# A fused transformer step on one core: coefficients of the expert rows computed on one engine instead of two

## The chip, the core and the metric

The kernel runs on one core of one Trainium2 chip, in fp32 throughout. A core has five engines that run side by side and meet only through semaphores: TensorE (PE in the profile) multiplies matrices, VectorE (DVE) and ScalarE (ACT) do elementwise work, GpSimd (POOL) here only issues gathers, and SyncE (SP) issues the other transfers. 16 DMA engines carry all transfers. The metric is the device time of one execution in microseconds (us), median of three runs.

## The reference, cut to what matters

One layer of a decoder trunk for 512 prompt tokens and 8 sample tokens: projections, retention and block-sparse attention, cross-attention over 256 memory tokens, and then the part that fills two thirds of the time, the retrieval of single-neuron experts. Each token has 8 heads, each head picks 16 of 16384 experts, and each expert is one row of `u` and one of `v`, 1024 numbers each:

```python
top, sel = lax.top_k(cand, PEER_TOPK)
expert = jnp.take_along_axis(cidx, sel, axis=-1)
g = jax.nn.softmax(top, axis=-1)
act = jax.nn.gelu(jnp.einsum('cd,chkd->chk', xc, u[expert]).astype(jnp.float32))
return jnp.einsum('chk,chkd->cd', (g * act).astype(v.dtype), v[expert])
```

So for each token and each picked expert there is a dot product `s` with the `u` row, a coefficient g·gelu(s), and the `v` row is added with that coefficient. gelu is the tanh form: 0.5·s·(1 + tanh(0.79788·(s + 0.044715·s³))).

## The kernel before, in words

Tokens lie on the 128 partitions, in four prompt tiles and one sample tile of 8. `u` and `v` are stored side by side, so one indirect DMA (line 759) brings, for one slot (head and rank) and all 128 tokens of a tile, the `u` and the `v` row of each token's expert: 128 rows of 8 KB, 1 MB in all. There are 4·128 such gathers for the prompt and 8 for the sample tile, 520 in all. They land in a ring of 7 buffers, `ring[k]`. GpSimd issues them strictly in order, and a gather waits until the previous user of its buffer has raised `row_free[k]`.

The program is written as a loop over 260 pairs of gathers, `PAIRS`, in the same order on every engine. x counts the 8 pairs of a head from 0 to 7. For pair p, before the change:

- VectorE takes the two dot products of pair p (`dot`, line 2266; each is one instruction over 128x1024 and a short one that reads the sum out), and raises `dots_done` after the second.
- ScalarE squares the two sums (`pair_gelu`, line 1550), VectorE forms s·(1 + 0.044715·s²) and s times half the gate (`pair_argument`, lines 2272 and 2275), ScalarE takes the tanh (line 1553), and VectorE forms the coefficients (`pair_coefs`, line 2282). That last step stands behind the first dot product of pair p+1 in VectorE's program.
- The `v` rows are added on two engines. Of the 8 ranks in each half head, slots 0, 2, 4, 5 and 7 (`PE_ROWS`) go to TensorE, the others to VectorE. For TensorE, ScalarE scales an identity matrix by the coefficients (`value_weights`, line 1565) into one of 6 buffers, and TensorE multiplies it with the row in four matmul instructions (line 1338: two halves of 512 columns, and an fp32 matmul is two instructions), summing in PSUM. For VectorE it is one instruction over 128x1024 (`value_rows`, line 2300) that adds into `h`. Pairs x = 2 and x = 6 of a head have two TensorE rows, the others one of each kind.
- After 64 pairs a tile is complete, and `add_sum` (line 2312) adds the PSUM sum to `h`. TensorE's first row of the next tile waits for that.

Around the pairs each engine has two other streams. Between the dot products VectorE takes pieces of the routing of later heads (`take`), that is the top-16 searches. And behind every odd pair, each engine takes the next piece of a background program (`advance(steps, progress(p // 2))`): the rest of the attention for the sample tokens and for the last prompt tile. On these pieces ScalarE mostly copies what TensorE has put in PSUM, and TensorE waits for the copy, so the two work in step there. The background ends about two thirds of the way through the pairs. In the program of TensorE, pair p-1's rows and then the background piece stand in iteration p; in that of ScalarE, it is the scaled identities of pair p-1, then square and tanh of pair p, and then the background piece.

## Time and profile before

| what | us |
|---|---|
| median of three runs | 2437.39 (2437.17 to 2438.58) |
| the profiled execution, its own time | 2440.81 |
| its span, first to last instruction | 2439.0 |
| first expert gather issued at | 748.80 |
| DVE busy / PE busy / POOL busy / ACT busy | 1460.5 / 1732.5 / 720.9 / 517.3 |

The profiled execution is 1.8 us longer than its span and 3.4 us above the median of the runs. The page's slices show three regions: the projections and the prompt's attention up to about 740 us, the pairs with background work up to about 1850 us, and the pairs with little beside them but routing up to the end. Busy time is the time in which an engine has an instruction in work; waiting for a semaphore is not counted.

### The profile page before, as it was taken

Reading aid. Unit: us, or ns where it says so; the run is one execution under the profiler, and the core shown is the slowest. Engines: PE = TensorE matmul, PEld = TensorE weight load, DVE = VectorE, ACT = ScalarE, POOL = GpSimd, SP = SyncE. Lnnn points to the kernel's source line nnn. Section 1 sums busy time; section 2 is a strip of 40 time slices with the busy share of each in tenths; the row PEclk is TensorE's granted clock in tenths of the full one; section 3 lists DMA queues with packets and bytes.
Section 4 is the critical chain, followed back from the end, with each engine's and each line's share of the span. In section 5 each row is a group of like instructions: output and inputs, shape, how many; then the busy total and the mean of one; then the engine's idle time right before and its main releaser. Section 6 shows DMA issues by size and latency. Waiting matters only on the chain.

```text
span 2439.0 us, 19114 instructions
## 1 busy us (share of the span) xinstructions
PE 1732.5 (71%) x5401; PEld 815.7 (33%) x5401; DVE 1460.5 (60%) x4222; ACT 517.3 (21%) x1533; POOL 720.9 (30%) x560
## 2 busy tenths in 40 slices
PE   5999998789783795796466666775765655566565
PEld 2333775435451231443122322441431222122221
DVE  2200037611215767547956785766877899999876
ACT  2000234512320231121112122111121211111212
POOL 0000000000005335423422343333433455554542
PEclk9999968989795898677778888777886667777778
DMA  6110600053018879968896997988999998999997
GB/s 211 69 69 35 205 6 1 20 179 141 1 67 312 306 297 390 374 255 293 308 384 278 388 374 297 364 349 335 385 374 403 375 366 348 358 368 381 374 401 294
DMA packets 124976, 654.41 MB, mean 268 GB/s; under 512 B 22960, under 2 KB 34256, under 8 KB 56928
## 3 DMA queue, kind: packets, MB, share of 16 engines
q0 software_dynamic: 78016, 562.07, 59.0%
q1 hardware_dynamic: 41816, 82.86, 9.9%
q10 hardware_dynamic: 5040, 8.26, 1.0%
q8 instruction: 44, 0.72, 0.1%
q14 instruction: 60, 0.49, 0.1%
HBM read 642.78 MB, written 14.55 MB: 270 GB/s over the span
## 4 chain that ended last, share of the span: by engine, by line
PE 41%; DMA 19%; issue 16%; DVE 13%; POOL 7%; ACT 4%; SPq 1%; ACTq 0%; POOLq 0%; DVEq 0%
DMA arena<-in_peer_uv,expert 17%; PE bank L1338 12%; PE bank L804 9%; POOL arena L759 6%; DVE arena L2266 3%; PE bank L1004 3%; DVE arena L2300 2%; PE bank L1089 2%; PE bank L1194 2%; PE bank L1228 2%; PE bank L1070 1%; PE bank L1121 1%; POOL arena L735 1%; PE bank L1205 1%; PE bank L826 1%
## 5 line engine op out<-in xcount | busy, mean ns | idle before, releaser
L1338 PE MATMUL bank<-arena 128*128 128x512 f32 (+1 forms) x1312 | 849.8, 797 | 579.9 <-ACT arena L1565 536.0
L759 POOL DMA_INDIRECT arena<-in_peer_uv,expert x512 | 671.4, 1311 | 946.9 <-PE bank L1338 785.9
L2266 DVE CUSTOM_DVE_ANT_0 arena<-arena 128x1024 f32<-128x1024 f32 x520 | 635.1, 1221 | 272.6 <-DMA arena<-in_peer_uv,expert 263.0
L1338 PEld LDWEIGHTS bank<-arena 128*128 128x128 f32 (+1 forms) x1312 | 300.1, 246 | 1104.8 <-issue 1104.3
L2300 DVE SCALAR_TENSOR_TENSOR arena<-arena 128x1024 f32<-128x1024 f32 x192 | 244.2, 1272 | 0.5
L804 PE MATMUL bank<-arena 128*128 128x512 f32 (+3 forms) x560 | 227.5, 565 | 0.0
L1565 ACT ACTIVATE arena<-arena 128x128 f32<-128x128 f32 x320 | 121.5, 399 | 407.1 <-DVE arena L2282 405.3
L1550 ACT ACTIVATE arena<-arena 128x2 f32<-128x2 f32 x260 | 53.1, 204 | 638.8 <-DVE arena L2266 638.8
L735 POOL DMA_INDIRECT arena<-in_cache_slc_k,row_idx x16 | 15.1, 946 | 444.0 <-DMA sc_scores<-arena 439.4
L804 PEld LDWEIGHTS bank<-arena 128*128 128x128 f32 (+1 forms) x560 | 93.6, 169 | 133.4 <-issue 128.3
L1763 DVE TENSOR_TENSOR arena<-arena 128x256 f32<-128x256 f32 (+5 forms) x20 | 6.4, 320 | 197.2 <-ACT arena L1411 197.2
L2272 DVE SCALAR_TENSOR_TENSOR arena<-arena 128x2 f32<-128x2 f32 x260 | 39.9, 153 | 79.4 <-ACT arena L1550 77.6
L1004 PE MATMUL bank<-arena 128*128 128x512 f32 (+1 forms) x160 | 72.3, 611 | 14.7 <-DMA arena<-in_w_out 12.0
L1553 ACT ACTIVATE arena<-arena 128x2 f32<-128x2 f32 x260 | 53.3, 205 | 123.9 <-DVE arena L2272 123.8
L728 POOL DMA_INDIRECT arena<-in_cache_cmp_k,blk_idx x2 | 2.0, 1023 | 243.0 <-PE bank L804 243.0
L2137 DVE MAX8 arena<-arena 128x8 f32<-128x128 f32 (+3 forms) x120 | 35.9, 326 | 48.8 <-ACT arena L1533 48.2
L1411 ACT ACTIVATE arena<-bank 128x512 f32<-128x512 f32 (+3 forms) x35 | 20.0, 570 | 207.6 <-PE bank L804 207.6
L1089 PE MATMUL bank<-arena 128*128 128x384 f32 (+1 forms) x256 | 58.2, 383 | 1.2 <-ACT arena L1391 1.2
L1968 DVE TENSOR_REDUCE arena<-bank 128x1 f32<-128x256 f32 (+1 forms) x17 | 7.2, 423 | 86.2 <-PE bank L1031 81.0
L1194 PE MATMUL bank<-arena 64*64 64x512 f32 x96 | 50.9, 614 | 0.5 <-ACT arena L1641 0.5
L1089 PEld LDWEIGHTS bank<-arena 128*128 128x128 f32 x256 | 40.6, 191 | 22.6 <-issue 5.7
L785 PE MATMUL bank<-arena 128*128 128x128 f32 (+1 forms) x136 | 23.6, 325 | 32.6 <-DVE arena L1746 27.8
(283 smaller groups left out, 1938.7 us busy)
## 6 DMA issues: line engine op xcount, KB each, us to landing
arena<-in_w_in SPq DMA_DIRECT2D x6, 2048.0 KB, 7.7
arena<-in_w_out SPq DMA_DIRECT2D x2, 4096.0 KB, 23.6
arena<-in_peer_uv,expert POOLq DMA_INDIRECT x512, 8.9
arena<-in_w_mq SPq DMA_DIRECT2D x2, 2048.0 KB, 10.7
arena<-in_peer_wq SPq DMA_DIRECT2D x2, 2048.0 KB, 10.7
arena<-in_w_mo SPq DMA_DIRECT2D x2, 2048.0 KB, 17.5
sc_scores<-arena ACTq DMA_DIRECT2D x4, 1024.0 KB
arena<-in_cache_mem_k SPq DMA_DIRECT2D x2, 2048.0 KB, 11.0
```

The lines of the kernel that those rows point to most:

```text
L759: pool.indirect_dma_start(out=ring[k], out_offset=None, in_=a["peer_uv"], in_offset=bass.IndirectOffsetOnAxis(ap=idx, axis=0)).then_inc(ro ...
L804: ins = pe.matmul(bank[0:R, 0:w], hnT[:, k, t * P:t * P + R], w_last[:, k, :] if last else w_buf[:, i % 2, k, 0:w], start=(k == 0), stop=( ...
L1004: ins = pe.matmul(bank[0:R, :], grp.catT[t][:, k, 0:R], grp.w_out[:, k, half * 512:(half + 1) * 512], start=(k == 0), stop=(k == KC - 1))
L1089: ins = pe.matmul(bank[:, 0:grp.width], grp.wq[:, k, hh * P:(hh + 1) * P], grp.hnT[:, k, :], start=(k == 0), stop=(k == KC - 1))
L1194: ins = pe.matmul(banks[4 + cc][0:64, :], q_mask[0:HD, bg, :], keyT[0:HD, gi % 2, :], start=(bg == 0), stop=(bg == BG - 1))
L1228: ins = pe.matmul(bank[0:HD, bg * R4:(bg + 1) * R4], vals[:, bg, j * HD:(j + 1) * HD], s_probsT[:, j, bg * R4:(bg + 1) * R4], start=(j == ...
L1338: ins = pe.matmul(banks[b + half][0:R, :], weights, ring[k][:, D + half * 512:D + (half + 1) * 512], start=first, stop=last)
L1550: act.activation(gelu_w[:, c0:c0 + 2], act_p[:, c0:c0 + 2], ACT.Square, scale=GELU_A ** 0.5).then_inc(act_squared, 1)
L1553: act.activation(gelu_w[:, c0:c0 + 2], gelu_w[:, c0:c0 + 2], ACT.Tanh, scale=GELU_B).then_inc(gelu_tanh, 1)
L1565: act.activation(diag[:, d % DIAGS, :], ident, ACT.Copy, scale=coef[:, slot:slot + 1]).then_inc(diag_ready, 1)
L2266: return dve.tensor_tensor_reduce(out=ring[k][:, 0:D], in0=ring[k][:, 0:D], in1=other, scale=1.0, scalar=0.0, op0=ALU.mult, op1=ALU.add, a ...
L2300: stt(out=h[:, n // H, :], in0=ring[k][:, D:2 * D], scalar=coef[:, c:c + 1], in1=h[:, n // H, :], op0=ALU.mult, op1=ALU.add).then_inc(row_ ...
```

## The change

The whole chain from dot products to coefficients moves to ScalarE. Square and tanh stay as instructions over two columns. The products with per-token factors become activations over one column each, with a column of SBUF as scale, and where something is added, as bias: the product s·half_gate is Copy with scale half_gate; s·(1 + 0.044715·s²) is Identity of the square with scale s and bias s; the coefficient is Identity of the tanh with scale and bias s·half_gate. That is 8 ScalarE instructions for a pair in place of 2, with four waits of ScalarE for its own results (`coef_step`, `coef_ready`), and none on VectorE in place of 3.

ScalarE then makes the scaled identities of the same pair at once, and TensorE's rows of pair p stand in iteration p and no longer in p+1. VectorE's rows stand where they did, behind the first dot product of the next pair. For the sample pairs the masked weights `coef_m` are made on ScalarE too. `add_sum` comes after pair x = 0 of the next tile and no longer after x = 1. `gates_made` tells ScalarE that the gates of a head are there.

```diff
@@ TensorE
-                    pe.wait_ge(diag_ready, diags[0])
+                weighted[0] += 1
+                pe.wait_ge(diag_ready, weighted[0])
...
-                if p:
-                    pair_values(p - 1, *PAIRS[p - 1])
+                pair_values(p, n, x)
                 if p % 2:
                     advance(steps, progress(p // 2))
-            pair_values(p, n, x)
@@ ScalarE
-            def pair_gelu(p, n, x):
+            def pair_coefs(p, n, x):
                 c0 = n % H * TOPK + 2 * x if n < HEADS else SLOTS + 2 * x
+                each = [slice(c, c + 1) for c in (c0, c0 + 1)]
+                if x == 0:
+                    act.wait_ge(gates_made, n + 1)
                 act.wait_ge(dots_done, p + 1)
-                act.activation(gelu_w[:, c0:c0 + 2], act_p[:, c0:c0 + 2], ACT.Square, scale=GELU_A ** 0.5
-                               ).then_inc(act_squared, 1)
-                act.wait_ge(gelu_in, p + 1)
-                act.activation(gelu_w[:, c0:c0 + 2], gelu_w[:, c0:c0 + 2], ACT.Tanh, scale=GELU_B
-                               ).then_inc(gelu_tanh, 1)
+                mark(act.activation(gelu_w[:, c0:c0 + 2], act_p[:, c0:c0 + 2], ACT.Square, scale=GELU_A ** 0.5))
+                for c in each:
+                    ins = act.activation(gated_x[:, c], act_p[:, c], ACT.Copy, scale=half_gate[:, c])
+                mark(ins)
+                act.wait_ge(coef_step, marks[0] - 1)
+                for c in each:
+                    ins = act.activation(gelu_w[:, c], gelu_w[:, c], ACT.Identity, scale=act_p[:, c], bias=act_p[:, c])
+                mark(ins)
+                act.wait_ge(coef_step, marks[0])
+                mark(act.activation(gelu_w[:, c0:c0 + 2], gelu_w[:, c0:c0 + 2], ACT.Tanh, scale=GELU_B))
+                act.wait_ge(coef_step, marks[0])
+                for c in each:
+                    ins = act.activation(coef[:, c], gelu_w[:, c], ACT.Identity, scale=gated_x[:, c], bias=gated_x[:, c])
+                ins.then_inc(coef_ready, 1)
...
-                if p:
-                    value_weights(p - 1, *PAIRS[p - 1])
-                pair_gelu(p, n, x)
+                pair_coefs(p, n, x)
+                value_weights(p, n, x)
@@ VectorE (pair_argument and pair_coefs are removed)
                 if x == 0 and n % H == 0 and 0 < n < HEADS:
                     t = n // H
+                    dve.wait_ge(dots_done, p)
...
-                if p:
-                    pair_coefs(p - 1, *previous)
                 take(before + (x + 0.5) * share)
                 if p:
                     value_rows(p - 1, *previous)
...
-                pair_argument(p, n, x)
                 previous = (n, x)
-                if n % H == 0 and 0 < n < HEADS and x == 1:
+                if n % H == 0 and 0 < n < HEADS and x == 0:
                     add_sum(n // H - 1)
```

ScalarE's program at a piece of background work in which it copies four banks of transposed keys for TensorE (line 1641 before, 1660 after; one row of x8 is two such pieces), before the change. L1550 is the square, L1553 the tanh, L1565 a scaled identity:

```order
L1550 ACTIVATE arena<-arena 128x2 [waits dots_done]
L1553 ACTIVATE arena<-arena 128x2 [waits gelu_in]
L1641 ACTIVATE arena<-bank 64x512 [waits s_keyT_done] x8
L1565 ACTIVATE arena<-arena 128x128 [waits row_free6,coef_ready]
L1550 ACTIVATE arena<-arena 128x2 [waits dots_done]
L1553 ACTIVATE arena<-arena 128x2 [waits gelu_in]
```

The same place after it. L1556 is the square, L1558 the product with the gate, L1562 the argument, L1565 the tanh, L1568 the coefficient, L1584 the scaled identity:

```order
L1556 ACTIVATE arena<-arena 128x2 [waits dots_done]
L1558 ACTIVATE arena<-arena 128x1 x2
L1562 ACTIVATE arena<-arena 128x1 [waits coef_step]
L1562 ACTIVATE arena<-arena 128x1
L1565 ACTIVATE arena<-arena 128x2 [waits coef_step]
L1568 ACTIVATE arena<-arena 128x1 [waits coef_step]
L1568 ACTIVATE arena<-arena 128x1
L1584 ACTIVATE arena<-arena 128x128 [waits row_free6,coef_ready]
L1660 ACTIVATE arena<-bank 64x512 [waits s_keyT_done] x8
```

The scaled identity of the odd pair stood behind the background copies and now stands ahead of them; the next pair's whole chain now stands behind them.

VectorE's program at the start of the third prompt tile, before the change. L2266 is a dot product, L2272, L2275 and L2282 are the small steps, L2300 is a row of VectorE, L2312 is `add_sum`:

```order
L2272 SCALAR_TENSOR_TENSOR arena<-arena 128x2 [waits act_squared]
L2275 TENSOR_TENSOR arena<-arena 128x2 [waits gate_step]
L2266 ISA arena<-arena 128x1024 [waits row_in6]
L2266 ISA arena 128x1
L2282 SCALAR_TENSOR_TENSOR arena<-arena 128x2 [waits gate_step,gelu_tanh]
L2148 MAX arena<-arena 128x8 [waits route_step]
L2148 MAX arena<-arena 128x8
L2300 SCALAR_TENSOR_TENSOR arena<-arena 128x1024 [waits row_free2,coef_ready]
...
L2312 TENSOR_TENSOR arena<-arena,bank 128x512 [waits row_free3,row_free2]
```

The same place after it, where L2283 is the dot product, L2297 VectorE's row and L2309 `add_sum`:

```order
L2309 TENSOR_TENSOR arena<-arena,bank 128x512 [waits row_free3,row_free2]
L2309 TENSOR_TENSOR arena<-arena,bank 128x512
L2283 ISA arena<-arena 128x1024 [waits row_in6]
L2283 ISA arena 128x1
L2165 MAX arena<-arena 128x8 [waits route_step]
L2165 MAX arena<-arena 128x8
L2297 SCALAR_TENSOR_TENSOR arena<-arena 128x1024 [waits row_free2,coef_ready]
```

The three small steps are gone, and `add_sum` stands ahead of the dot product into buffer 6 and no longer behind that of buffer 0.

## Rows read from the trace of the kernel before

**Rows 1.** Windows view; busy us per engine, clock, DMA share, GB/s of two stretches.

```profile
740.00:1850.00 1110.00, 744.58 (x2171) 335.41 (x2171) 765.56 (x2148) 216.10 (x706) 417.63 (x343) 0.78 0.87 339
1850.00:2345.00 495.00, 298.50 (x438) 106.20 (x438) 450.93 (x1393) 87.11 (x316) 260.46 (x174) 0.73 0.97 372
```

**Rows 2.** Waits, 740 to 1850: engine, line, awaited; us in total, times, longest.

```profile
POOL arena L759 <- PE bank L1338: 575.6, 140, 32.2
ACT arena L1565 <- DVE arena L2282: 262.5, 127, 17.4
DVE arena L2266 <- DMA arena<-in_peer_uv,expert: 213.5, 131, 30.1
DVE arena L2272 <- ACT arena L1550: 72.6, 15, 15.6
ACT arena L1553 <- DVE arena L2272: 63.8, 154, 1.4
```

**Rows 3.** Waits, 1850 to 2345.

```profile
POOL arena L759 <- PE bank L1338: 201.0, 78, 13.5
ACT arena L1565 <- DVE arena L2282: 123.8, 85, 3.4
ACT arena L1553 <- DVE arena L2272: 56.8, 85, 1.2
DVE arena L2266 <- DMA arena<-in_peer_uv,expert: 37.3, 48, 2.3
```

**Rows 4.** Timeline, one pair late on: start us, us, engine, instruction.

```profile
2224.74 0.20 ACT L1550 ACTIVATE arena<-arena 128x2 f32<-128x2 f32 x1 [2.60 <-DVE arena L2266]
...
2225.64 0.14 DVE L2275 TENSOR_TENSOR arena<-arena 128x2 f32<-128x2 f32 x1
2225.71 1.21 DVE L2266 CUSTOM_DVE_ANT_0 arena<-arena 128x1024 f32<-128x1024 f32 x1
...
2226.86 0.14 DVE L2282 SCALAR_TENSOR_TENSOR arena<-arena 128x2 f32<-128x2 f32 x1
2226.93 0.74 DVE L2188 TENSOR_TENSOR arena<-arena 8x256 f32<-8x256 f32 x2
2227.04 0.69 ACT L1565 ACTIVATE arena<-arena 128x128 f32<-128x128 f32 x2 [1.09 <-DVE arena L2282]
```

**Rows 5.** ScalarE: line 1380, an activation over one column, min/median/max ns.

```profile
L1380 ACT ACTIVATE arena<-arena x22: 293/294/296, 23.5 to 2434.0; 128x1 f32<-128x1 f32 x18, 8x1 f32<-8x1 f32 x4
```

**Rows 6.** Timeline, two turns with background work between TensorE and ScalarE.

```profile
881.32 5.68 PE L1338 MATMUL bank<-arena 128*128 128x512 f32 x12
...
886.84 0.60 PE L1205 MATMUL bank<-arena 128*64 128x128 f32 x4
...
892.15 0.59 ACT L1641 ACTIVATE arena<-bank 64x512 f32<-64x512 f32 x1 [0.96 <-PE bank L1205]
892.64 0.39 ACT L1565 ACTIVATE arena<-arena 128x128 f32<-128x128 f32 x1
892.93 0.19 ACT L1550 ACTIVATE arena<-arena 128x2 f32<-128x2 f32 x1
893.18 3.97 PE L1338 MATMUL bank<-arena 128*128 128x512 f32 x8
893.35 0.20 ACT L1553 ACTIVATE arena<-arena 128x2 f32<-128x2 f32 x1 [0.23 <-DVE arena L2272]
893.46 0.20 ACT L1540 ACTIVATE arena<-arena 128x16 f32<-128x16 f32 x1
```

**Rows 7.** Timeline, the start of the second tile.

```profile
1215.81 0.15 DVE L2272 SCALAR_TENSOR_TENSOR arena<-arena 128x2 f32<-128x2 f32 x1
...
1225.83 5.08 PE L1338 MATMUL bank<-arena 128*128 128x512 f32 x8 [10.43 <-DVE arena L2312]
```

**Rows 8.** Chain that ended last: start us, us, what; the two longest background pieces shown.

```profile
1021.96 27.41 PE bank L1228 x256
...
1639.40 15.03 PE bank L1070 x32
```

More of the change, by code:

```diff
@@ L498, in trunk_kernel @@
         route_step = sem("route_step")
-        act_squared = sem("act_squared")
+        coef_step = sem("coef_step")
+        gates_made = sem("gates_made")
         gate_step = sem("gate_step")
-        gelu_in = sem("gelu_in")
-        gelu_tanh = sem("gelu_tanh")
         x_done = sem("x_done")
@@ L1316, in background @@
                 yield STEPS_DONE
-            diags = [0]
+            diags, weighted = [0], [0]
             def value_row(p, n, x, y):
@@ L1327, in value_row @@
                     weights, first, last = coef_m[:, j, :], j == 0, j == DB - 1
-                    pe.wait_ge(coef_ready, p + 1)
                 else:
@@ L1545, in sample_exp, with mark @@
                 act.activation(best_v[0:DB, :], best_v[0:DB, :], ACT.Exp).then_inc(sample_gate, 1)
-            def pair_gelu(p, n, x):
+            marks = [0]
+            def mark(ins):
+                ins.then_inc(coef_step, 1)
+                marks[0] += 1
+            def pair_coefs(p, n, x):
                 c0 = n % H * TOPK + 2 * x if n < HEADS else SLOTS + 2 * x
+                each = [slice(c, c + 1) for c in (c0, c0 + 1)]
+                if x == 0:
+                    act.wait_ge(gates_made, n + 1)
@@ L1556, in _ @@
+                act.wait_ge(coef_step, marks[0])
+                for c in each:
+                    ins = act.activation(coef[:, c], gelu_w[:, c], ACT.Identity, scale=gated_x[:, c], bias=gated_x[:, c])
+                ins.then_inc(coef_ready, 1)
             diags, diag_user = [0], []
             def value_weights(p, n, x):
+                act.wait_ge(coef_ready, p + 1)
                 for y in range(2):
-                    if n < HEADS and PE_PART[n, x, y]:
+                    if n == HEADS:
+                        j = 2 * x + y
+                        act.activation(coef_m[:, j, :], eye8[:, j, :], ACT.Copy, scale=coef[:, SLOTS + j:SLOTS + j + 1]
+                                       ).then_inc(diag_ready, 1)
+                    elif PE_PART[n, x, y]:
@@ L1561, in value_weights @@
                         d, slot = diags[0], n % H * TOPK + 2 * x + y
-                        act.wait_ge(coef_ready, p + 1)
                         if d >= DIAGS:
@@ L1724, in _ @@
                     mean_square(h[0:DB, SAMPLE, :], hn3[:, SAMPLE, :], x_done, 1)
-            value_weights(p, n, x)
             mean_square(h[:, PT - 1, :], hn3[:, 3, :], sum_added, 2 * PT)
@@ L2226, in sample_columns @@
                 dve.wait_ge(rt_done, 1)
-                order(dve.tensor_copy(half_gate[:, SLOTS:SLOTS + DB], banks[0][:, DB:2 * DB]))
+                dve.tensor_copy(half_gate[:, SLOTS:SLOTS + DB], banks[0][:, DB:2 * DB]).then_inc(gates_made, 1)
                 dve.tensor_copy(expert_s[:, :], banks[0][:, 0:DB]).then_inc(idx_ready, 1)
@@ L2232, in final_norm @@
                 normed(h[:, t, :], h[0:R, t, :], gain[:, 0, :]).then_inc(y_ready, 1)
-            gates, x_marked = [0], {}
+            gates = [0]
             def gate_mark(ins):
@@ L2252, in head_gates @@
                 dve.wait_ge(gate_step, gates[0])
-                gate_mark(ts(half_gate[:, cols], best_e[:, cols], scale, None, ALU.mult))
+                ts(half_gate[:, cols], best_e[:, cols], scale, None, ALU.mult).then_inc(gates_made, 1)
                 yield
@@ L2267, in dot @@
                                                 scalar=0.0, op0=ALU.mult, op1=ALU.add, accum_out=act_p[:, c:c + 1])
-            def pair_argument(p, n, x):
-                cols = pair_cols(n, x)
-                dve.wait_ge(act_squared, p + 1)
-                stt(out=gelu_w[:, cols], in0=gelu_w[:, cols], scalar=1.0, in1=act_p[:, cols], op0=ALU.add, op1=ALU.mult
-                    ).then_inc(gelu_in, 1)
-                dve.wait_ge(gate_step, gates[0])
-                gate_mark(tt(gated_x[:, cols], act_p[:, cols], half_gate[:, cols], ALU.mult))
-                x_marked[p] = gates[0]
-            def pair_coefs(p, n, x):
-                cols = pair_cols(n, x)
-                dve.wait_ge(gelu_tanh, p + 1)
-                dve.wait_ge(gate_step, x_marked[p])
-                ins = stt(out=coef[:, cols], in0=gelu_w[:, cols], scalar=1.0, in1=gated_x[:, cols], op0=ALU.add, op1=ALU.mult)
-                if n == HEADS:
-                    order(ins)
-                    ins = tt(coef_m[:, 2 * x:2 * x + 2, :], eye8[:, 2 * x:2 * x + 2, :],
-                             coef[:, cols].unsqueeze(2).broadcast_to((P, 2, DB)), ALU.mult)
-                ins.then_inc(coef_ready, 1)
             last_row = []
@@ L2380, in _ @@
                     final_norm(SAMPLE)
-            pair_coefs(p, *previous)
             value_rows(p, *previous)
```

## The prediction, made before the changed kernel ran

> **What bounds the kernel now.** I read the page first: the projections and the prompt's attention, up to 740 us, are untouched, so I cut the rest into stretches with the windows view [rows 1]. The first stretch, 740 to 1850, holds some 158 pairs (316 of the 343 GpSimd instructions, the others being page gathers of the attention), 7.0 us each; no engine is full (DVE 69%, PE 67%) and the DMA engines moved 339 GB/s. The second, 1850 to 2345, holds 87 pairs (174 gathers), 5.7 us each, with VectorE busy 451 of 495 us and the DMA engines at 0.97 and 372 GB/s. Then the waits. In the first stretch GpSimd waited 576 us for TensorE to free a ring buffer, and VectorE 214 us for gathers to land [rows 2]: the ring is the bound, a circle of gather, dot products, coefficients, TensorE's row, next gather. Seven buffers at 3.5 us a row make a circle of 24.6 us. In the second stretch VectorE lost only 37 us to gathers [rows 3]: there it is the bound itself, with a nearly full DMA right behind it.
>
> In that circle the part that the change touches is the time from square to scaled identity. From the waits: 0.20 (square) + wait of the tanh for VectorE + 0.20 (tanh) + wait of the identity for VectorE. Second stretch: 0.20 + 56.8/85 + 0.20 + 123.8/85 = 2.5 us [rows 3]; the pair shown has 2.30, of which 1.2 us is the first dot product of the next pair, standing ahead of the coefficients [rows 4]. First stretch: 0.20 + 63.8/154 + 0.20 + 262.5/127 = 2.9 us [rows 2], and more for an odd pair, whose identity stands behind a background piece as well.
>
> **The new chain, step by step.** Neither an activation over one column with two column operands nor ScalarE waiting for itself stands in the trace. Line 1380 takes one column operand over one column: 294 ns [rows 5]. An activation over two columns without one takes 200 [rows 4], so a column operand adds some 90, and I take 385 for two. Independent activations start about 0.1 us before the one ahead ends (893.35 + 0.20 against 893.46 [rows 6]). A dependent one I start 0.05 after the end. Then: square to 0.20; two Copies started at 0.11 and 0.30, to 0.59; two Identities at 0.49 and 0.77, to 1.15; tanh 1.20 to 1.40; two Identities at 1.45 and 1.73, to 2.11; identity matrix at 2.15. Bounds: if column operands cost nothing it is about 1.25; with no overlap anywhere, 0.2 + 0.59 + 0.77 + 0.2 + 0.77 + 0.2 of handing over = 2.75. I take 2.15.
>
> The Trainium skill says the same of the operands (ScalarE: Activation LUTs, What ACT_TABLE_LOAD costs): an activation with immediate scale and bias takes 186 ns and each pointer operand adds about 93. By that page the two-operand form would take an estimated 373 ns and the chain about 2.1 us. It speaks against the change: the chain is longer in instruction time than the old one, and only its place is better.
>
> So the chain is about 0.4 us shorter than the average old one in the second stretch, and at most level with the shortest old ones.
>
> **What it is worth, place by place.**
>
> *VectorE's three small steps.* They start 0.07 us apart and the next instruction 0.07 behind [rows 4], so each takes 0.07 from the engine and not its 0.15: 0.21 us a pair. In the second stretch, where VectorE is the bound, 87 x 0.21 = 18 us. VectorE's row needs the coefficients 2.11 after the square; it reaches that place after the next first dot, which in the pair shown ended 2.2 after it, and a routing piece of up to 0.75 more [rows 4]. So there is no new stall on average, but only 0.1 to 0.8 of margin. Gathers then have to run at 372 x 5.7/5.5 = 386 GB/s. I take 18, and bound it by 0 (DMA full already) and 18 + 37 (landing waits gone as well). Of those 37 us, an earlier release by 0.4 in a circle of 20 us gives back some 5. Second stretch: -23.
>
> *Tile starts, three.* TensorE's first row waited for `add_sum`, which stood behind the second pair: idle 10.4 us at 1225.8 [rows 7]. The first pair's argument was formed at 1215.8; now its coefficients are there at about 1217, and `add_sum` (two instructions of 0.7 us) runs at 1215.8 to 1217.1. So the row starts some 8 us sooner. The ring covers part of that; I take 5 us each, -15 in all, between 0 and 3 x 8.
>
> *First stretch, release of odd pairs.* The odd pair's rows now come ahead of the background piece on both engines. For an identity that waited behind it the gain is 2 us or more; averaged with the even pairs, which gain little, 1.1 us in a circle of 24.6 us, 4.5%. Over some 800 us of the stretch, 1110 less 12 turns of 12 us [rows 6] and seven of about 24, this is -36 us, bounded by 0 and, if every wait of VectorE for a gather went, by 214.
>
> *First stretch, turns in which TensorE and ScalarE work in step.* Here the change costs. In the turn shown the rows of three slots take 5.7 us, the background piece 6.3, and TensorE is never idle: its next row starts 0.5 us after ScalarE's last copy, since the odd pair's coefficients were made by VectorE meanwhile [rows 6]. Now the pair behind the piece is an even one whose whole chain stands behind ScalarE's copies: TensorE idles 2.15 us more. There are 12 such pieces of key copies (16·8/4 + 16·4/4 = 48 copies of line 1641, in fours): +26. Behind the long pieces, of which I count seven in the code's steps (the two shown took 27 and 15 us on TensorE [rows 8]), the same chain is exposed: +15. Also, each piece now starts on TensorE later against the dot products (behind pair p's rows instead of pair p-1's), so ScalarE is held longer. VectorE no longer stops at the next square for that (72.6 us in 15 waits [rows 2]) but at the next row, some 3 us further on; I set the one against the other, at 0.
>
> *VectorE's small steps in the first stretch* lie beside its waits for gathers: 0, at best 158 x 0.21 = 33.
>
> *The end.* Behind the last dot products nothing hid the old chain, 0.2 + 0.15 + 0.2 + 0.15 and four hand-overs, 0.9 us; now 2.15: +1.
>
> Sum: -23 - 15 - 36 + 26 + 15 + 1 = -32. The profiled span of 2439.0 would become 2407, its execution 2409, and the median, 3.4 us lower than that execution, **2405**.
>
> **Rivals.**
>
> *A larger gain.* The ring is the bound of the first stretch and everything on it counts in full: the exposed chains are covered by the extra pair in flight, the small steps give 33 there, and the landing waits shrink. -23 - 24 - 36 - 33 + 1 = -115 at the most; half way from my sum, **2365**. For it speak the 576 us that GpSimd waited for TensorE [rows 2]. Against it speak the DMA engines at 0.87 already.
>
> *No change.* In the second stretch the DMA engines are full at 0.97 [rows 1], so VectorE's gain becomes landing wait, and the first stretch's gains and costs meet at zero: within 5 us of **2437**. Against it speaks that no stretch has shown a sharp limit at 372 GB/s.
>
> *Slower.* One mechanism: ScalarE is held in a background piece until TensorE has done pair p's rows and the piece, and the next pair's coefficients begin only then. Before, the piece could start while pair p's dot products were still running. It starts now 2.65 us (chain and identity) and a row of 1.9 us or more behind them, some 4 us later. The pair period is 7 us; once a piece takes more than about 2.5 us, the next square is late and TensorE idles for the chain in every such turn. If it decides in 40 of the 79 turns and not in 12, it costs 40 x 2.15 = 86 in place of 26, and the odd pairs' gain is used up too (the even pair is late by as much): -23 - 15 + 86 + 15 + 1 = +64, less what the ring absorbs, about half: **2469**. It would decide from about 25 turns on. The even distribution of small pieces speaks for it, against it that the ring holds three and a half pairs.
>
> That the change does not do what it says is little likely: the order on each engine shows the chain and the moved rows. Identity is not among the functions that the kernel used; the number of table loads in the order is unchanged.
>
> **How the numbers follow.** The forecast has 0.46, the larger gain 0.20, no change 0.11, slower 0.23. The forecast's own range is 2385 to 2428. The range of 2368 to 2462 leaves out the outer half of the larger gain and a part of the slower case. A difference under 0.2% (5 us) is about what a measurement of this kernel can't tell from none. Faster: 0.46 x 0.98 + 0.20 = 0.65. Within: 0.12. Slower: 0.23.
>
> **What would show it.** In the profile after: square to scaled identity 2.1 to 2.2 us in all but background turns, with the two-operand activations near 385 ns; VectorE's 3 x 260 small instructions gone; its period in the second stretch 5.4 to 5.5 us a pair, at 380 GB/s or more; a new wait of line 2297 for ScalarE, under 10 us in the second stretch; TensorE's wait for `add_sum` at the tile starts nearly gone; in the background turns TensorE idle some 2.7 us behind the last copy. The forecast is wrong if the first stretch is more than 10 us longer than before, if the new wait of VectorE for coefficients passes 40 us in all, or if the second stretch keeps its 5.7 us a pair.

## The result and the profile after

| | before | changed |
|---|---|---|
| median, us | 2437.96 (2437.17 to 2438.58, 4 runs) | 2509.1 (2499.19 to 2521.07, 4 runs) |
| ratio | | 1.0309, 95% interval 1.0268 to 1.0351 |
| span of the profiled execution | 2439.0 | 2511.2 |

The change makes the kernel 3.1% slower, where 1.3% faster was forecast; the time also lies outside the range. All ratios here and below compare executions in the chip's usual state; one of the kernel before, in the second set of experiments, took 3176 us at a lower granted clock and is left out.

The first look is at where the 72 us of the span arose. I take the end of the second dot product of each pair as a clock: pair 0 ends at 759.4 us before and 752.8 after, pair 160 at 1863.5 and 1947.1, pair 240 at 2323.1 and 2394.1, pair 256 at 2407.7 and 2480.2. So 90 us were lost over the 160 pairs with background work, and 12.5 us were won over the 80 pairs behind them. Pair 0 is 6.6 us sooner, which says nothing of the change: over all runs of this document it ends between 752.6 and 765.0.

The same stretches in the windows view of the changed kernel (columns as in [rows 1]):

```profile
740.00:1850.00 1110.00, 720.25 (x1984) 321.07 (x1985) 680.22 (x1566) 433.71 (x1528) 383.13 (x314) 0.75 0.81 311
1850.00:2345.00 495.00, 293.10 (x554) 112.96 (x553) 425.45 (x1124) 221.50 (x826) 247.38 (x171) 0.78 0.97 376
```

ScalarE has over twice the work. TensorE, VectorE, GpSimd and the DMA engines (311 GB/s in place of 339) are all less busy in the first stretch than before: nobody there is fuller but ScalarE, at 39%, and everyone waits more. The stretch also holds fewer pairs than before. Over the same pairs, 0 to 160, the first number behind the comma is TensorE's busy time; first before, then the changed kernel:

```profile
759.40:1863.50 1104.10, 753.53 (x2187) 338.87 (x2187) 773.43 (x2166) 218.42 (x714) 410.26 (x334) 0.79 0.87 341
```

```profile
752.80:1947.10 1194.30, 778.33 (x2187) 350.76 (x2187) 735.97 (x1687) 473.66 (x1674) 409.45 (x335) 0.76 0.82 316
```

The same 2187 TensorE instructions take 25 us more, at a granted clock of 0.76 in place of 0.79, and TensorE is idle for 416 us in place of 351. Those 25 and 65 us are the 90. The waits of the changed kernel, 740 to 1850 us, against [rows 2]:

```profile
POOL arena L758 <- PE bank L1337: 529.4, 131, 29.1
PE bank L1337 <- ACT arena L1584: 382.9, 105, 40.6
DVE arena L2283 <- DMA arena<-in_peer_uv,expert: 183.5, 106, 29.2
POOL arena L758 <- DVE arena L2297: 142.1, 22, 28.6
DVE arena L2297 <- ACT arena L1568: 130.6, 25, 18.1
```

Two rows of the kernel before that belong beside them, from the same view:

```profile
PE bank L1338 <- ACT arena L1565: 325.9, 105, 41.7
POOL arena L759 <- DVE arena L2300: 42.0, 15, 9.3
```

And 1850 to 2345 us, against [rows 3]:

```profile
POOL arena L758 <- PE bank L1337: 189.8, 77, 8.7
DVE arena L2283 <- DMA arena<-in_peer_uv,expert: 55.3, 55, 11.8
DVE arena L2297 <- ACT arena L1568: 9.7, 4, 5.2
```

The new wait is that of VectorE's row (line 2297) for coefficients that ScalarE had not made: 131 us in 25 waits in the first stretch, where VectorE used to lose 73 us in 15 waits at the square [rows 2], and 10 us in the second. GpSimd waits for VectorE's rows 142 us, before 42. TensorE's wait for scaled identities, the largest that it has, grew from 326 to 383 us.

The new chain itself came out as worked out. One pair in the stretch without background, to be read against [rows 4]; L1556 is the square, L1558 two products, L1562 two arguments, L1565 the tanh, L1568 two coefficients, L1584 the scaled identity:

```profile
2135.15 0.21 ACT L1556 ACTIVATE arena<-arena 128x2 f32<-128x2 f32 x1 [4.04 <-DVE arena L2283]
2135.26 0.46 ACT L1558 ACTIVATE arena<-arena 128x1 f32<-128x1 f32 x2
2135.63 0.65 ACT L1562 ACTIVATE arena<-arena 128x1 f32<-128x1 f32 x2
2136.31 0.21 ACT L1565 ACTIVATE arena<-arena 128x2 f32<-128x2 f32 x1
2136.55 0.66 ACT L1568 ACTIVATE arena<-arena 128x1 f32<-128x1 f32 x2
2137.24 0.40 ACT L1584 ACTIVATE arena<-arena 128x128 f32<-128x128 f32 x1
```

2.09 us from square to identity, 2.15 predicted; the median over pairs 158 to 244 is 2.10. The two forms with two column operands (min/median/max ns), against [rows 5]:

```profile
L1562 ACT ACTIVATE arena<-arena x520: 370/372/380, 753.8 to 2496.8; 128x1 f32<-128x1 f32 x174
L1568 ACT ACTIVATE arena<-arena x520: 370/380/389, 754.8 to 2497.7; 128x1 f32<-128x1 f32 x174
```

What went wrong is in a turn with background work. The timeline of the changed kernel, to be read against [rows 6]; L1204 is the start of TensorE's piece of key transposes, L1660 ScalarE's copies, the last of a piece shown:

```profile
896.65 0.59 ACT L1660 ACTIVATE arena<-bank 64x512 f32<-64x512 f32 x1 [0.97 <-PE bank L1204]
897.15 0.19 ACT L1556 ACTIVATE arena<-arena 128x2 f32<-128x2 f32 x1
...
899.78 8.33 PE L1337 MATMUL bank<-arena 128*128 128x512 f32 x12 [2.16 <-ACT arena L1584]
...
907.95 0.60 PE L1204 MATMUL bank<-arena 128*64 128x128 f32 x4
...
913.26 0.59 ACT L1660 ACTIVATE arena<-bank 64x512 f32<-64x512 f32 x1 [0.97 <-PE bank L1204]
913.75 0.19 ACT L1556 ACTIVATE arena<-arena 128x2 f32<-128x2 f32 x1
915.83 0.40 ACT L1584 ACTIVATE arena<-arena 128x128 f32<-128x128 f32 x1
915.83 1.28 DVE L2297 SCALAR_TENSOR_TENSOR arena<-arena 128x1024 f32<-128x1024 f32 x1 [10.10 <-ACT arena L1568]
916.38 3.43 PE L1337 MATMUL bank<-arena 128*128 128x512 f32 x4 [2.16 <-ACT arena L1584]
```

From first row to first row the turn takes 16.6 us; before it took 11.9 (881.32 to 893.18, [rows 6]). TensorE idles 2.16 us for a whole chain behind the piece, as the prediction priced it, but the three rows also take 8.3 us in place of 5.7. The windows view of the two turns (PEclk is the third number from the end) says more; first before, then the changed kernel:

```profile
881.30:893.20 11.90, 11.76 (x37) 4.42 (x37) 8.22 (x25) 4.07 (x11) 7.18 (x5) 1.00 0.84 310
```

```profile
899.70:916.40 16.70, 14.46 (x37) 5.61 (x37) 4.43 (x10) 7.34 (x25) 4.15 (x4) 0.81 0.77 291
```

Before, TensorE worked through the turn and had the full clock, 1.00; now it stands idle once and does part of the turn at the lower of its two levels. The first 3.2 us behind the idle time, in which it is busy throughout:

```profile
899.80:903.00 3.20, 3.20 (x4) 1.47 (x5) 1.08 (x1) 2.42 (x10) 0.00 (x0) 0.50 0.64 269
```

2.2 us of idle time and 2.6 us of slower rows make the 4.7 us of this turn. In the same turn VectorE stood for 10.1 us at its row, with the next dot products behind it.

Over all pairs up to 155, a square starts more than 0.3 us after its dot products 16 times before and 39 times in the changed kernel, and these delays add up to 78 and 231 us. Before, TensorE never stood idle for more than 0.1 us ahead of the first row of such a late pair. In the changed kernel it does so 24 times, for 1.7 to 6.1 us and 64 us in all: these are nearly the whole of the 65 us of added idle time.

### The profile page after: what moved, and what is told of

The parts are those of the page before. It is cut to its first block, busy times and chain, and to the rows that moved or that the text cites. A ratio compares the mean times of both kernels' runs of the same rounds, so it can differ in the third digit from the quotient of the medians.

```text
span 2511.2 us, 19608 instructions
## 1 busy us (share of the span) xinstructions
PE 1740.5 (69%) x5401; PEld 819.3 (33%) x5401; DVE 1399.0 (56%) x3438; ACT 933.5 (37%) x3101; POOL 710.7 (28%) x560
## 4 chain that ended last, share of the span: by engine, by line
PE 44%; DMA 16%; DVE 14%; ACT 10%; issue 10%; POOL 5%; SPq 1%; ACTq 0%; POOLq 0%; DVEq 0%
PE bank L1337 14%; DMA arena<-in_peer_uv,expert 13%; PE bank L803 9%; DVE arena L2283 5%; POOL arena L758 4%; DVE arena L2297 3%; PE bank L1003 3%; PE bank L1088 2%; ACT arena L1562 2%; PE bank L1193 2%; PE bank L1069 1%; PE bank L1227 1%; ACT arena L1568 1%; ACT arena L1558 1%; PE bank L1020 1%
## 5 line engine op out<-in xcount | busy, mean ns | idle before, releaser
L1337 PE MATMUL bank<-arena 128*128 128x512 f32 (+1 forms) x1312 | 864.4, 812 | 645.1 <-ACT arena L1584 636.6
L2283 DVE CUSTOM_DVE_ANT_0 arena<-arena 128x1024 f32<-128x1024 f32 x520 | 634.5, 1220 | 284.8 <-DMA arena<-in_peer_uv,expert 273.6
L1337 PEld LDWEIGHTS bank<-arena 128*128 128x128 f32 (+1 forms) x1312 | 307.7, 250 | 1177.5 <-issue 1177.1
L2297 DVE SCALAR_TENSOR_TENSOR arena<-arena 128x1024 f32<-128x1024 f32 x192 | 244.6, 1274 | 143.3 <-ACT arena L1568 143.0
L1556 ACT ACTIVATE arena<-arena 128x2 f32<-128x2 f32 x260 | 52.8, 203 | 721.6 <-DVE arena L2283 691.0
L1568 ACT ACTIVATE arena<-arena 128x1 f32<-128x1 f32 x520 | 172.8, 379 | 8.7
L1562 ACT ACTIVATE arena<-arena 128x1 f32<-128x1 f32 x520 | 169.0, 372 | 0.0
L734 POOL DMA_INDIRECT arena<-in_cache_slc_k,row_idx x16 | 15.1, 946 | 437.2 <-DMA sc_scores<-arena 432.6
L803 PEld LDWEIGHTS bank<-arena 128*128 128x128 f32 (+1 forms) x560 | 93.6, 169 | 133.4 <-issue 128.3
L1584 ACT ACTIVATE arena<-arena 128x128 f32<-128x128 f32 x320 | 121.9, 400 | 8.3
L1558 ACT ACTIVATE arena<-arena 128x1 f32<-128x1 f32 x520 | 120.8, 279 | 0.0
L1003 PE MATMUL bank<-arena 128*128 128x512 f32 (+1 forms) x160 | 71.5, 605 | 14.6 <-DMA arena<-in_w_out 11.9
L1565 ACT ACTIVATE arena<-arena 128x2 f32<-128x2 f32 x260 | 53.3, 205 | 8.0
L1660 ACT ACTIVATE arena<-bank 64x512 f32<-64x512 f32 x48 | 28.2, 592 | 75.1 <-PE bank L1204 75.1
```

Source lines behind the costliest of these rows:

```text
L803: ins = pe.matmul(bank[0:R, 0:w], hnT[:, k, t * P:t * P + R], w_last[:, k, :] if last else w_buf[:, i % 2, k, 0:w], start=(k == 0), stop=( ...
L1003: ins = pe.matmul(bank[0:R, :], grp.catT[t][:, k, 0:R], grp.w_out[:, k, half * 512:(half + 1) * 512], start=(k == 0), stop=(k == KC - 1))
L1337: ins = pe.matmul(banks[b + half][0:R, :], weights, ring[k][:, D + half * 512:D + (half + 1) * 512], start=first, stop=last)
L1558: ins = act.activation(gated_x[:, c], act_p[:, c], ACT.Copy, scale=half_gate[:, c])
L1562: ins = act.activation(gelu_w[:, c], gelu_w[:, c], ACT.Identity, scale=act_p[:, c], bias=act_p[:, c])
L1565: mark(act.activation(gelu_w[:, c0:c0 + 2], gelu_w[:, c0:c0 + 2], ACT.Tanh, scale=GELU_B))
```

## The experiments

Theory A: what costs is the order against the background, a chain exposed behind each piece. Theory B: the ScalarE chain costs wherever it stands. The kernel before ran beside each set below on that set's chip: medians of 2432.4, 2431.1 and 2434.7 us for the three sets, with single runs spread wider (2416 to 2449) than in the result above. So kernels of different sets are compared by their ratios. Where a text counts time from pair to pair, it is that of one profiled execution of each kernel.

**Only TensorE's piece moved back.** In the changed kernel:

```diff
@@ TensorE
+                if p % 2:
+                    advance(steps, progress(p // 2))
                 pair_values(p, n, x)
-                if p % 2:
-                    advance(steps, progress(p // 2))
```

> The changed kernel, with TensorE's background piece of an odd pair ahead of that pair's rows again (ScalarE unchanged: chain and scaled identities, then its piece). Theory A (order): the loss of the changed kernel sits where TensorE's piece, behind pair p's rows, starts only after pair p's dot products and chain, so that ScalarE is held and the next pair's whole chain is exposed behind the piece. Then this kernel gives the 90 us of the background stretch back and keeps the 13 us won in the stretch without background: 2410 to 2430 us, late squares back from 39 to about 16. Theory B (load and length): the 2.1 us chain of 8 ScalarE instructions itself costs, wherever TensorE's pieces stand: 2480 us or more.

Measured: 2442.6 us, ratio 1.0032 (1.0000 to 1.0064). That is 13 us above the range that I expected, but nearly the whole loss is gone by moving one engine's piece back ahead of the rows. Squares that start over 0.3 us after their dot products, 16 before and 39 in the changed kernel, are 22, and TensorE stands idle behind them 5 times in place of 24.

**The ScalarE chain with identities and TensorE's rows in the old place.**

```diff
@@ TensorE
+                if p:
+                    pair_values(p - 1, *PAIRS[p - 1])
-                pair_values(p, n, x)
@@ ScalarE
+                if p:
+                    value_weights(p - 1, *PAIRS[p - 1])
                 pair_coefs(p, n, x)
-                value_weights(p, n, x)
```

> The chain is on ScalarE, but scaled identities and TensorE's rows of pair p stand in iteration p+1, so behind the background piece of an odd pair on both engines, as before the change. Theory A: 2415 to 2435 us, a little slower than the kernel with only TensorE's piece moved, since the identity of an odd pair is late by the piece. Theory B: 2480 us or more.

Measured: 2434.7 us, ratio 1.0003 (0.9975 to 1.0031). Two turns of TensorE in its trace, the counterpart of the two above:

```profile
885.41 1.96 PE L1337 MATMUL bank<-arena 128*128 128x512 f32 x4
887.80 3.67 PE L1337 MATMUL bank<-arena 128*128 128x512 f32 x8 [0.43 <-ACT arena L1586]
891.31 0.60 PE L1204 MATMUL bank<-arena 128*64 128x128 f32 x4
...
897.64 1.96 PE L1337 MATMUL bank<-arena 128*128 128x512 f32 x4
```

The row behind the piece is that of the odd pair, whose coefficients were made ahead of the piece. The turn takes 12.2 us and the clock stays up, at 1.00: three rows in 5.6 us. ScalarE does all the work here that it does in the changed kernel, so Theory B is out. Against the kernel before, this one is 16 us late by pair 96 and makes it up again: from pair 160 to 240 it takes 444.9 us, before 459.6, changed kernel 447.1. But the run above, whose chain is the same too, takes 454.0, and the one with only the earlier sum, below, takes 453.2 with the old chain. So what the new chain wins in the late stretch is not told well by single executions: 6 to 15 us against before, and nothing clear against the run with the earlier sum.

**The piece ahead of the pair on both engines.** ScalarE's `advance` also moves ahead of `pair_coefs(p, n, x)`.

> The changed kernel, with the background piece ahead of the pair on both TensorE and ScalarE, so that the chain of the odd pair stands behind the piece instead of that of the even pair. Theory A in its narrow form (what costs is a whole chain behind a piece, with TensorE idle for it once in every background turn): little better than the changed kernel, 2450 to 2490 us, and clearly slower than the kernel with only TensorE's piece moved. If only the late start of the piece on TensorE costs, 2410 to 2430 us as there. Theory B: 2480 us or more.

Measured: 2527.1 us, ratio 1.0384 (1.0339 to 1.0428), slower than I expected of it and no better than the changed kernel. Here TensorE's piece starts as early as before the change, and only the chain stands behind it (now that of the odd pair; 42 late squares). So the late start of the piece is not the cause by itself: what counts is that no pair's coefficients are ready when the piece ends. TensorE stands idle behind such a late pair 39 times, for 125 us in all, against 24 times and 64 us in the changed kernel.

**Only the earlier tile sum**, in the kernel before: `x == 1` becomes `x == 0` at `add_sum`.

> The kernel before, with the one edit that the tile sums are added after pair x = 0 instead of x = 1. The prediction's step: 5 us at each of three tile starts, 2420 to 2430 us. Rival: TensorE's rows and the gathers behind them are covered by the ring, or wait for the coefficients as before, since these still stand behind the next pair's first dot product: 2435 to 2440 us.

Measured: 2430.3 us, ratio 0.9979 (0.9952 to 1.0006). Not told apart from no change; the 15 us (0.994) of the prediction are outside the interval. TensorE's idle time ahead of the first rows of the three tiles shrank from 10.4, 15.1 and 9.1 us to 4.4, 9.8 and 5.5 here, 15 us in all, and the time by some 5 at the median. In the changed kernel the idle time at the second tile's start did shrink, from 10.43 us [rows 7] to 2.13:

```profile
1258.03 1.27 DVE L2309 TENSOR_TENSOR arena<-arena,bank 128x512 f32<-128x512 f32 x2
1259.25 0.40 ACT L1584 ACTIVATE arena<-arena 128x128 f32<-128x128 f32 x1
1259.80 2.88 PE L1337 MATMUL bank<-arena 128*128 128x512 f32 x4 [2.13 <-ACT arena L1584]
```

With theory A shown in the main, the question was why the new chain wins so little elsewhere, and what its length is worth.

**A short chain in the changed kernel.** The coefficients are not the reference's here:

```diff
-                for c in each:
-                    ins = act.activation(gated_x[:, c], act_p[:, c], ACT.Copy, scale=half_gate[:, c])
+                ins = act.activation(gated_x[:, c0:c0 + 2], act_p[:, c0:c0 + 2], ACT.Copy)
...
-                for c in each:
-                    ins = act.activation(gelu_w[:, c], gelu_w[:, c], ACT.Identity, scale=act_p[:, c], bias=act_p[:, c])
+                ins = act.activation(gelu_w[:, c0:c0 + 2], gelu_w[:, c0:c0 + 2], ACT.Copy, scale=0.5)
...
-                for c in each:
-                    ins = act.activation(coef[:, c], gelu_w[:, c], ACT.Identity, scale=gated_x[:, c], bias=gated_x[:, c])
+                ins = act.activation(coef[:, c0:c0 + 2], gelu_w[:, c0:c0 + 2], ACT.Copy, scale=0.001)
```

> The changed kernel with its chain cut short: the six activations over one column with column operands become three over two columns with none (Copy in place of the product with the gate, of the argument and of the coefficient), so the coefficients are not the reference's; order, waits and everything else stay. The chain falls from 2.1 to about 1.0 us. Theory A (a whole chain stands behind each background piece): 39 late turns by 1.1 us give back about 43 us of the 84 lost in the background stretch, 2455 to 2475 us; what stays is the late start of TensorE's piece. If the length hardly counts: 2495 us or more. If it is all: 2430 us or less.

Measured: 2407.1 us, ratio 0.9893 (0.9860 to 0.9926): 4.2% off the changed kernel's ratio, 101 us, over twice what I expected, and more than all of the loss. The chain is 0.94 us, for instance:

```profile
2136.91 0.20 ACT L1556 ACTIVATE arena<-arena 128x2 f32<-128x2 f32 x1 [4.39 <-DVE arena L2280]
...
2137.85 0.40 ACT L1581 ACTIVATE arena<-arena 128x128 f32<-128x128 f32 x1
```

**The same short chain in the old place.**

> The same short chain (wrong coefficients again) in the kernel that has its scaled identities and TensorE's rows in the old place. With the full chain that kernel was level with before: about 16 us lost over the heavy background turns and 15 won in the stretch without background. If the loss there is the chain's length on ScalarE, the short chain gives it back: 2405 to 2420 us. If the stretch without background is bound by the ring, its period falls below the 5.56 us a pair of the full chain, to about 5.4; if by the DMA engines, it stays within 0.05 of it.

Measured: 2369.9 us, ratio 0.9757 (0.9715 to 0.9799). 1.15 us less of chain saves 2.5%, 60 us, where no piece stands between: not only the 16 us of the background turns that I expected, but something in every pair. From pair 160 to 240 it takes 431.0 us, 5.39 a pair against 5.56, and VectorE has the same work in both. In the changed kernel's order the short chain wins as much there, 434.2 against 447.1. So VectorE alone did not set the period.

**The old chain while there is background, the changed one behind it** (pairs 0 to 155 and 156 to 259; with the earlier tile sum).

> The old two-engine chain in its old place for pairs 0 to 155, as long as there is background work, and the changed chain, in its new place, for pairs 156 to 259; tile sums a pair sooner throughout. Theory A: no loss in the background stretch, the 13 us of the stretch without background and some 3 of the earlier sum: 0.992 to 0.996 of the kernel before, about 2415 to 2422 us where that has 2432. If the gain of the late stretch in the changed kernel was only that of a kernel that had fallen behind (other transfers out of the way): 0.999 to 1.002.

Measured: 2423.1 us, ratio 0.9958 (0.9934 to 0.9982). The changed chain where no background is behind it, with the earlier tile sum, makes the kernel 0.4% faster, about 10 us, as expected. In its profiled execution 7.1 us of it came between pairs 160 and 240, but the kernel with only the earlier sum is 6.4 us ahead of before in the same pairs. What the chain won there, and what the earlier sum, is not shown.

**Six ring buffers in place of seven**, in the kernel before (`RING = 6`). Theory C, which the expectations name from here on: the ring's circle of gather, dot products, coefficients and row sets the period in the late stretch too.

> The kernel before with 6 ring buffers in place of 7. Theory C: the circle of gather, dots, coefficients, row is of fixed length, so the period grows by up to 7/6: from 5.7 to 6.3 to 6.6 us a pair in the stretch without background, and the whole by 120 us or more. My prediction's reading, that VectorE is the bound there: the period stays within 5.9 us, and the whole grows by under 60 us, from the first stretch.

Measured: 2639.1 us, ratio 1.0838 (1.0784 to 1.0891). From pair 160 to 240 it takes 525.2 us, 6.57 a pair against 5.75: times 1.143, where 7/6 would be 1.167. In the windows view its stretch 1850 to 2345 has VectorE at 379 us and 326 GB/s; below it, for comparison, the short chain in the old place:

```profile
1850.00:2345.00 495.00, 273.70 (x528) 108.01 (x526) 379.01 (x1162) 75.80 (x276) 184.59 (x147) 0.75 0.88 326
```

```profile
1850.00:2345.00 495.00, 303.62 (x475) 105.61 (x474) 441.50 (x1122) 133.93 (x617) 266.73 (x184) 0.78 0.99 396
```

Three and a half pairs of 5.75 make a circle of 20.1 us, three of 6.57 make 19.7. So the circle sets the period with six buffers, and with seven it is as long as the period too. That it is then the only bound does not follow. The circle is not of fixed length either: the time from square to identity grew from 2.6 to 3.35 us late on, since the coefficients stand behind the next pair's first dot product, and VectorE's dot products waited 111 us for gathers in this stretch, before 37 [rows 3]. And 1.15 us less of chain would by the ring alone give 1.15/3.5 = 0.33 us a pair; 0.17 came late on, and 0.23 over all 260 pairs. VectorE's work, the gathers and the ring are close to balance there. Nor was 0.97 a full DMA: 396 GB/s are to be had.

**A chain shared by what is short where.** Square on ScalarE and argument and gate product on VectorE, as before the change; then tanh and the two coefficients on ScalarE, so that they no longer stand behind the next dot product. Identities and TensorE's rows in the old place:

```diff
@@ ScalarE
                 mark(act.activation(gelu_w[:, c0:c0 + 2], act_p[:, c0:c0 + 2], ACT.Square, scale=GELU_A ** 0.5))
+                act.wait_ge(gelu_in, 2 * p + 1)
                 mark(act.activation(gelu_w[:, c0:c0 + 2], gelu_w[:, c0:c0 + 2], ACT.Tanh, scale=GELU_B))
                 act.wait_ge(coef_step, marks[0])
+                act.wait_ge(gelu_in, 2 * p + 2)
                 for c in each:
                     ins = act.activation(coef[:, c], gelu_w[:, c], ACT.Identity, scale=gated_x[:, c], bias=gated_x[:, c])
```

> A chain shared out by what each engine is short of, with scaled identities and TensorE's rows in the old place: square on ScalarE, argument and gate product on VectorE behind its routing piece (as before the change), tanh and then the two coefficients on ScalarE, with column scale and bias (as in the changed kernel), so no longer behind VectorE's next dot product. Chain: 0.25 + the wait for VectorE of 0.4 to 0.7 + 0.25 + 0.7 = about 1.6 to 1.8 us. Theory C (the ring: every microsecond of chain costs 260/3.5 = 74 us at most; measured in the old place 65 us for 1.15 us of chain): 0.3 to 0.5 us less than the kernel with the ScalarE chain in the old place, 17 to 28 us faster than it: 2405 to 2418 us, 0.989 to 0.994 of before. If VectorE's two small steps count in full (260 times 0.14 = 36 us): no gain, 2430 to 2445 us.

Measured: 2401.0 us, ratio 0.9859 (0.9831 to 0.9887): 1.4% faster than before, somewhat better than expected, and the best of the kernels that compute the reference. It has the earlier tile sum as well. Of the 35 us by which it beats the ScalarE chain in the old place, 27 lie between pairs 0 and 160 and none between 160 and 240 (444.4 us). Its chain, late on, with VectorE's steps L2286 and L2289:

```profile
2138.71 0.21 ACT L1557 ACTIVATE arena<-arena 128x2 f32<-128x2 f32 x1 [3.50 <-DVE arena L2280]
...
2139.91 0.13 DVE L2286 SCALAR_TENSOR_TENSOR arena<-arena 128x2 f32<-128x2 f32 x1
2139.97 0.14 DVE L2289 TENSOR_TENSOR arena<-arena 128x2 f32<-128x2 f32 x1
2140.07 0.21 ACT L1559 ACTIVATE arena<-arena 128x2 f32<-128x2 f32 x1 [1.16 <-DVE arena L2286]
2140.31 0.67 ACT L1563 ACTIVATE arena<-arena 128x1 f32<-128x1 f32 x2
2140.80 1.23 DVE L2280 CUSTOM_DVE_ANT_0 arena<-arena 128x1024 f32<-128x1024 f32 x1 [0.69 <-DMA arena<-in_peer_uv,expert]
2141.01 0.40 ACT L1579 ACTIVATE arena<-arena 128x128 f32<-128x128 f32 x1
```

2.3 us here, because VectorE was in a routing piece; over the pairs 158 to 244 the mean is 1.9 (2.6 before), and the median of even pairs with background work 1.4. The identity no longer waits for the dot product at 2140.80, which came late from its gather.

**The same shared chain in the changed kernel's order.**

> The same shared chain in the changed kernel's order (identities and TensorE's rows ahead of the background piece). Theory A with its measured size, 79 us for a chain of 2.1 and 39 us for one of 0.95, so 35 background turns by the chain's length: 35 times 1.6 to 1.8 = 56 to 63 us over the same chain in the old order, 2460 to 2480 us. If the order costs a fixed 40 us: 2445 to 2455 us.

Measured: 2469.0 us, ratio 1.0146 (1.0111 to 1.0182): 2.9% over the old order. By ratios, the new order costs 3.1% or 74 us with the chain of 2.1 us, 2.9% or 70 us with the shared one of 1.6 to 1.8 (its means in even pairs with background work and late on), and 1.4% or 33 us with that of 0.94. A fixed price is excluded; some 35 turns by the length of the chain fit the first and the last, and the middle one (56 to 63 us by it) within the intervals. The 35 is fitted and not counted: in the traces TensorE stands idle behind a late pair 24, 24 and 19 times, for 64, 46 and 30 us. Its busy time up to pair 160 is 25 us above that in the old order with the chain of 2.1 us (778.3 against 753.5), and within 2 us of it with the other two. So the slower rows are a part of the longest chain's price alone.

## Why the prediction was wrong, step by step

- *What bounds the kernel.* For the first stretch the ring, right. For the second I read "VectorE busy 91%, 37 us of waits for gathers" as VectorE's bound. A shorter chain with VectorE's work unchanged took 13 to 14 us off the 80 pairs, so the circle counts there too, and the ring of six shows it as long as the period. VectorE and the circle were nearly in balance, and the GpSimd wait of 201 us in the same rows said so.
- *The chain.* 2.15 us worked out, 2.09 measured. The overlap of neighbours and the price of a column operand, both from rows of other lines, held.
- *Second stretch, -23.* 12.5 us in the profiled executions, over 80 of the 87 pairs, but single executions scatter there: the two kernels with the old chain and seven buffers took 459.6 and 453.2 us, the five with the new one of 2.1 us 444.9 to 454.0, by the means 7 us less. VectorE's freed time was there, 0.21 us a pair (busy 405.8 us in place of 422.5), but the period fell by less. The chain was shorter by 0.4 to 0.5 us, which at the rate of the short chain is 5 to 6 us. And TensorE's rows ran faster by chance or otherwise: 266.9 us busy in place of 275.3, at a granted clock of 0.77 in place of 0.73. How the gain divides among the three is not shown. The 5 us that the forecast took out of the landing waits do not follow from its own figures: 0.4 us over 3.5 pairs, times 87, is 10.
- *Tile starts, -15.* In the changed kernel the second tile's row waits 8 us less, as said. Alone, the earlier sum is worth some 5 us at the median, within noise, for 15 us less of idle time.
- *Odd pairs' earlier release, -36.* Not seen: the order that releases them sooner costs 74 us net. I had priced the early half of the turn and the late half apart and with different counts. What the term is alone was not tried, so it stays open.
- *Turns in which TensorE and ScalarE work in step, +26 and +15.* This is the step that failed. The mechanism was right, TensorE idle for 2.16 us behind the last copy, but its size was wrong. I had 19 turns (12 and 7) of 2.15 us, 41 us; it was 24 turns of 2.7 on average, 64 us, and 25 us of slower matmuls that the sum had at nothing, 89 us in all. In the turn shown, which grew by 4.7 us, the two parts were 2.2 and 2.6. The later start of TensorE's piece, with ScalarE held longer, was put at 0 without a measurement behind it: that VectorE's stop merely moves "some 3 us further on" and cancels was wrong. The delays of the squares tripled, 78 to 231 us, and VectorE's stops rose from 73 to 131 us, with single ones of up to 18 us.
- *The rival "slower"* named this mechanism and 40 deciding turns. It then halved the sum for what the ring absorbs, 2469. Unhalved it said +64; measured, +71. That these are close is partly luck: it had 40 turns of 2.15 us and 15 us for the long pieces, 101 us, where 24 longer turns and slower matmuls made 89, and it had -23 and -15 for terms that came out smaller. The halving was wrong: idle behind the pieces rose by 64 us and TensorE's whole idle time by 65, so in these traces nothing of it was absorbed. My likeliest case rested on the same ring as its bound and priced the same turns at 41 us instead of 101.
- *Of what would show it wrong*: the first stretch over 10 us longer, VectorE's new wait over 40 us. Both came.

What stays open: whether the piece ahead on both engines is slower still than the changed kernel (ratios 1.0384 and 1.0309, with intervals that just overlap; its trace has the more idle turns, 39 against 24), and how the 16 us lost over the first 96 pairs by the ScalarE chain in the old place divide among its turns. With the short chain the same kernel gains 14 us on before from pair 0 to pair 96, so the chain's length is in it; more was not tried.

## What to carry to other kernels

When a ring of buffers is a bound, price a change by the latency it puts on the circle, divided by the depth of the ring, beside the busy time it takes from the fullest engine, and take it as the most that it can be: here half to seven tenths of it came. A ring one buffer smaller tells in one run whether the circle is near the period. Where two engines work through a second stream in step, look at what is ready when a piece ends: keep one unit's results made ahead of the piece, so that the engine behind it has work at once. Work for a dependent chain belongs on the engine that is free at that moment of the turn, and sharing it out step by step can beat moving it as a whole.

## What the runs showed of the hardware that I had not expected

In the turn of the changed kernel shown above, a stop of 2.2 us doubled in price. The granted clock of that turn was 0.81 over 16.7 us, after and with two idle gaps of 2.16 us, and 0.50 right behind the first gap; three rows took 8.3 us. In the turns without such a gap it was 1.00, and three rows took 5.7 (before) and 5.6 us (chain in the old place, one gap of 0.43). Over all pairs up to 160 the slower matmuls were 25 of the 90 us. With 24 shorter stops, 46 us in all, as the shared chain has them in the same order, TensorE's busy time did not grow (751.1 us against 752.7 in the old order). The late stretch moved up to 396 GB/s at a DMA share of 0.99 with the short chain, where 372 at 0.97 had looked full.
